# Diagonal state space layer: the kernel matrix last on TensorE, the skip inside the states, block spreading and decay from GpSimd to ScalarE

## The reference, cut to what matters

```
bu_re = jnp.einsum('gpc,bsgc->bsgp', bb_re, uf)
bu_im = jnp.einsum('gpc,bsgc->bsgp', bb_im, uf)
...
_, _, xr, xi = lax.associative_scan(_complex_affine_combine, (a_r, a_i, bu_re, bu_im), axis=1)
y = (jnp.einsum('gcp,bsgp->bsgc', c_re.astype(f32), xr)
     - jnp.einsum('gcp,bsgp->bsgc', c_im.astype(f32), xi)
     + d.astype(f32).reshape(S5_GROUPS, S5_GROUP_CH) * uf)
...
g_a, g_b = jnp.split(jax.nn.gelu(y) @ od_w_glu[o], 2, axis=-1)
x = x + g_a * jax.nn.sigmoid(g_b)
```

## Time and profile before

| | |
|---|---|
| median of 3 runs | 2890.25 us (2887.17 to 2892.11) |
| the profiled execution's own time | 2897.58 us |
| its span, first to last instruction | 2895.8 us |
| busy: PE / DVE / ACT / POOL | 2560.8 / 1790.8 / 922.8 / 1552.7 us |
| the S5 stage, first VectorE product to last state | 2207.08 to 2368.77 us |

### The profile page before, as it was taken

How to read it: one execution, slowest core, us unless ns; L and a number is a source line. 1 busy time by engine, 2 the same in 40 slices (tenths; PEclk the granted TensorE clock), 3 DMA queues, 4 the chain that set the end, 5 groups by cost and what they waited for, 6 DMA issues and landing times.

```text
span 2895.8 us, 36385 instructions
## 1 busy us (share of the span) xinstructions
PE 2560.8 (88%) x12686; PEld 2003.5 (69%) x12686; DVE 1790.8 (62%) x2121; ACT 922.8 (32%) x1317; POOL 1552.7 (54%) x1274
## 2 busy tenths in 40 slices
PE   4978888969999997999588989999995559999998
PEld 3755677747777776778377458888883558888887
DVE  6669855656777675566788556664237763666314
ACT  2023266633444422667312213221022221222102
POOL 4730344535444452445464016766768757767775
PEclk8977899979999997999799689999997889999999
DMA  8846478852233223788431113332240013333222
GB/s 304 271 117 212 160 265 300 303 164 86 82 93 94 94 81 115 275 306 291 138 88 57 62 51 99 90 101 94 95 125 21 22 37 88 102 94 95 95 94 80
DMA packets 319121, 386.72 MB, mean 134 GB/s; under 512 B 51578, under 2 KB 259214, under 8 KB 318902
## 3 DMA queue, kind: packets, MB, share of 16 engines
q1 hardware_dynamic: 261424, 335.84, 35.4%
q10 hardware_dynamic: 34438, 28.08, 3.2%
q0 software_dynamic: 23168, 21.59, 2.3%
HBM read 397.62 MB, written 55.41 MB: 156 GB/s over the span
## 4 chain that ended last, share of the span: by engine, by line
PE 28%; POOL 20%; issue 20%; DVE 15%; DMA 12%; ACT 3%; SPq 1%; ACTq 0%; POOLq 0%; DVEq 0%
POOL WL L829 15%; PE PAIR L527 5%; POOL WH L825 5%; PE PAIR L528 5%; PE PAIR L529 5%; DMA RAW<-in_moe_w 5%; PE PAIR L1830 2%; DMA RAW<-in_ffn_w_up 2%; PE BANK L2260 2%; DVE WL L1932 2%; ACT WH L1750 1%; PE BANK L527 1%; PE BANK L528 1%; PE BANK L529 1%; PE PAIR L1800 1%
## 5 line engine op out<-in xcount | busy, mean ns | idle before, releaser
L829 POOL TENSOR_TENSOR WL<-RAW,WH 128x512 fp32r<-128x512 f32 x584 | 819.2, 1433 | 12.2
L527 PE MATMUL PAIR<-HH,WH 128*128 128x512 f32 x1792 | 714.1, 398 | 51.0 <-POOL HL L1118 30.5
L528 PE MATMUL PAIR<-HL,WH 128*128 128x512 f32 x1792 | 704.8, 393 | 0.0
L529 PE MATMUL PAIR<-HH,WL 128*128 128x512 f32 x1792 | 703.7, 393 | 0.0
L824 POOL TENSOR_TENSOR TURN<-ONES 128x1 f32<-128x1 f32 x146 | 34.6, 237 | 927.3 <-PE PAIR L529 850.4
L527 PEld LDWEIGHTS PAIR<-HH,WH 128*128 128x128 f32 x1792 | 340.3, 190 | 134.9 <-issue 45.0
L529 PEld LDWEIGHTS PAIR<-HH,WL 128*128 128x128 f32 x1792 | 340.5, 190 | 72.0
L528 PEld LDWEIGHTS PAIR<-HL,WH 128*128 128x128 f32 x1792 | 340.6, 190 | 71.3 <-issue 2.4
L825 POOL TENSOR_SCALAR WH<-RAW 128x2048 fp32r<-128x2048 f32 x146 | 281.1, 1925 | 0.0
L1932 DVE TENSOR_TENSOR WL<-RAW,WH 128x2048 fp32r<-128x2048 f32 x78 | 178.7, 2293 | 159.2 <-ACT WH L1750 159.2
L2002 POOL DMA_INDIRECT XG<-htok_scratch,GATHER_I x78 | 142.4, 1825 | 219.1 <-PE PAIR L1800 130.7
(11 more groups left out here) (518 smaller groups left out, 4653.5 us busy)
## 6 DMA issues: line engine op xcount, KB each, us to landing
RAW<-in_moe_w SPq DMA_DIRECT2D x156, 512.0 KB, 4.8
RAW<-in_ffn_w_up SPq DMA_DIRECT2D x88, 512.0 KB, 4.6
W2RAW<-in_moe_w SPq DMA_DIRECT2D x78, 512.0 KB, 6.6
ADA_B<-in_ada_w SPq DMA_DIRECT2D x30, 1024.0 KB, 5.3
RAW<-in_ssm_w_in SPq DMA_DIRECT2D x48, 512.0 KB, 4.9
ADA_A<-in_ada_w SPq DMA_DIRECT2D x18, 1024.0 KB, 7.9
RAW<-in_ffn_w_down SPq DMA_DIRECT2D x32, 512.0 KB, 4.0
RAW<-in_ev_w_in SPq DMA_DIRECT2D x20, 512.0 KB, 4.3
```

Source lines behind the costliest of these rows:

```text
L527: nc.tensor.matmul(o, wh, xh, start=start, stop=False)
L528: nc.tensor.matmul(o, wh, xl, start=False, stop=False)
L529: return nc.tensor.matmul(o, wl, xh, start=False, stop=stop)
L829: ins = pool.tensor_tensor(WL[:, s, c], RAW[:, s, c], WH[:, s, c].bitcast(F32), ALU.subtract)
```

## The change

On TensorE, `pe_s5_prepare` moves the inputs first, then transposes `W1X`, then computes B·u, and puts the kernel matrix last, in the fourth bank. On VectorE, the skip of step k-1 moves from behind the states of step k to a place inside them, between the scans and the last six operations. On GpSimd, sums and differences are taken in place on all 128 partitions (two for `W1_PR`, two for `PRP`), both of which now have two buffers; ScalarE copies them to their blocks (`act_s5_blocks`, eight copies of 64 partitions a step) and also computes `S5_DECAY` (`act_s5_decay`, four activations of 128x128 with a scale per partition). ScalarE's loop is written out. At the start ScalarE does the blocks of steps 0 and 1 before the inputs of step 0.

```
-    PRP = sb("PRP", [P, 4, 4, S5_L + 1, S5_C], F32, r)
-    W1_PR = sb("W1_PR", [P, 4, 4, S5_L, S5_C], F32, r)
+    W1_PR = sb("W1_PR", [P, 2, 4, 4, S5_L, S5_C], F32, r)
...
+    PRP = sb("PRP", [P, 2, 4, 4, S5_L + 1, S5_C], F32, r)
...
 def pool_s5_step(pool, k):
...
+        if k >= 2:
+            pool.e.wait_ge(w["w1x"], k - 1)
+        q = [W1_PR[:, par, i] for i in range(4)]
         for i, (a, b) in enumerate(((br, ar), (bi, ai), (br, ai), (bi, ar))):
-            ins = pool.e.tensor_tensor(W1_PR[:, i], a, b, ALU.mult)
+            ins = pool.e.tensor_tensor(q[i], a, b, ALU.mult)
         pool.link(ins)
-        if k >= 2:
-            pool.e.wait_ge(bank_ready, s5_a(k - 2, 2) + 1)
-        for part, op in ((0, ALU.subtract), (1, ALU.add)):
-            for h in range(2):
-                rows = slice(h * HD, h * HD + HD)
-                ins = pool.e.tensor_tensor(W1X[rows, par, part, :, :, h, :], W1_PR[rows, 2 * part], W1_PR[rows, 2 * part + 1], op)
-        ins.then_inc(w["w1x"], 1)
-        pool.wait(w["w1x"])
+        pool.e.tensor_tensor(q[0], q[0], q[1], ALU.subtract)
+        pool.e.tensor_tensor(q[2], q[2], q[3], ALU.add).then_inc(w["w1_sums"], 1)
+        pool.wait(w["w1_sums"])
...
+        if k >= 2:
+            pool.e.wait_ge(w["ca"], k - 1)
+        q = [PRP[:, par, i] for i in range(4)]
...
+        pool.e.tensor_tensor(q[0], q[0], q[1], ALU.subtract)
+        pool.e.tensor_tensor(q[2], q[2], q[3], ALU.subtract).then_inc(w["ca_sums"], 1)
+        pool.wait(w["ca_sums"])
...
-        pool.e.tensor_tensor(S5_DECAY[:, par], bcast(FIRST[:], 1, 4), bcast(S5K[:, MAG4, tiles], 2, S5_N), ALU.mult)\
-            .then_inc(w["decays"], 1)
...
+    def act_s5_blocks(act, k):
+        w, par = s5_sems, k % 2
+        act.wait(w["w1_sums"])
+        if k >= 2:
+            act.e.wait_ge(bank_ready, s5_a(k - 2, 3) + 1)
+        for part in range(2):
+            for h in range(2):
+                rows = slice(h * HD, h * HD + HD)
+                ins = act.e.activation(W1X[rows, par, part, :, :, h, :], W1_PR[rows, par, 2 * part], ACT.Copy)
+        ins.then_inc(w["w1x"], 1)
+        act.wait(w["ca_sums"])
+        if k >= 2:
+            act.e.wait_ge(bank_ready, s5_y(k - 2) + 1)
+        for part in range(2):
+            for h in range(2):
+                rows = slice(h * HD, h * HD + HD)
+                ins = act.e.activation(CAX[rows, par, part, :, :, h, :], PRP[rows, par, 2 * part], ACT.Copy)
+        ins.then_inc(w["ca"], 1)
+
+    def act_s5_decay(act, k):
+        w, par = s5_sems, k % 2
+        if k >= 2:
+            act.e.wait_ge(w["state"], k - 1)
+        for i in range(4):
+            ins = act.e.activation(S5_DECAY[:, par, i, :], FIRST[:], ACT.Identity, scale=S5K[:, MAG4, 4 * k + i:4 * k + i + 1])
+        ins.then_inc(w["decays"], 1)
...
+        act_s5_decay(act, 0)
+        act_s5_blocks(act, 0)
+        act_s5_blocks(act, 1)
+        act_s5_inputs(act, 0)
+        act_s5_kernel(act, 0)
+        for k in range(KD):
+            if k < KD - 1:
+                act_s5_decay(act, k + 1)
+                act_s5_inputs(act, k + 1)
+            if k:
+                act_s5_gelu(act, None, k - 1)
+            if k < KD - 1:
+                act_s5_kernel(act, k + 1)
+            act_s5_output(act, None, k)
+            if k + 2 < KD:
+                act_s5_blocks(act, k + 2)
+        act_s5_gelu(act, None, KD - 1)
...
 def dve_s5_states(dve, e, k):
...
             ins = dve.e.tensor_tensor_scan(q[i + 1], decay, q[i], 0.0, ALU.mult, ALU.add)
         dve.link(ins)
         if e is not None or k:
+            dve_s5_skip(dve, e, k - 1)
...
             dve_s5_states(dve, e, k)
-            if e is not None or k:
-                dve_s5_skip(dve, e, k - 1)
```

`act_s5_inputs` copies the inputs (bank 0) and the two transposed banks (1 and 2), and `act_s5_kernel` the kernel matrix (bank 3). TensorE's new order, with the waits:

```
+        bank = take_bank(pe, s5_a(k, 0))
...
+        pe.wait(w["w1x"])
         for part in range(2):
+            bank = take_bank(pe, s5_a(k, 1 + part))
...
+        for i in (0, 1, 2):
+            b = s5_a(k, i)
+            pe.e.wait_ge(bank_free[b % 4], b // 4 + 1)
...
+        pe.wait(w["ca"])
+        bank = take_bank(pe, s5_a(k, 3))
```

More of the change, by code:

```diff
@@ L3184, in s5_out @@
         return s5_y(k) + 1
[L3186 to L3194, removed]
     def t2(e, n):
@@ L3285, in pool_s5, with pe_s5_prepare @@
             pool_s5_step(pool, k)
-    def pe_s5_prepare(pe, e, k):
+    def pe_s5_prepare(pe, k):
         w, par = s5_sems, k % 2
+        bank = take_bank(pe, s5_a(k, 0))
+        for i in range(4):
+            for j in range(S5_L):
+                src = HF[:, k:k + 1, :].rearrange("p k (n l) -> p (k n) l", l=S5_L)[:, :, j]
+                ins = nc.tensor.matmul(bank[32 * j:32 * j + 32, i * P:i * P + P], IDENT[:, 32 * i:32 * i + 32], src, start=True, stop=True)
+        ins.then_inc(bank_ready, 1)
         pe.wait(w["w1x"])
         for part in range(2):
-            bank = take_bank(pe, s5_a(k, part), t2(e, 3))
+            bank = take_bank(pe, s5_a(k, 1 + part))
             for i in range(4):
@@ L3296, in pe_s5_prepare @@
             ins.then_inc(bank_ready, 1)
+        pair = take_pair(pe, plan.p["s5"] + k)
+        for i in (0, 1, 2):
+            b = s5_a(k, i)
+            pe.e.wait_ge(bank_free[b % 4], b // 4 + 1)
+        for part in range(2):
+            for i in range(4):
+                ins = nc.tensor.matmul(pair[:, part, i * P:i * P + P], W1_T[:, par, part, i, :], U4[:, par, i, :], start=True, stop=True)
+        ins.then_inc(w["bu"], 1)
         pe.wait(w["ca"])
-        bank = take_bank(pe, s5_a(k, 2), t2(e, 3))
+        bank = take_bank(pe, s5_a(k, 3))
         for i in range(4):
@@ L3303, in pe_s5_prepare @@
         ins.then_inc(bank_ready, 1)
[L3304 to L3317, removed]
     def pe_s5_output(pe, e, k):
@@ L3351, in pe_s5, with act_s5_inputs @@
         pe.wait(h_ready)
[L3353 to L3359, removed]
+        pe_s5_prepare(pe, 0)
         for k in range(KD):
-            step(None, k)
-    def act_s5_prepare(act, e, k):
+            if k < KD - 1:
+                pe_s5_prepare(pe, k + 1)
+            pe_s5_output(pe, None, k)
+    def act_s5_inputs(act, k):
         par = k % 2
         if k >= 2:
-            act.e.wait_ge(bank_ready, t2(e, 12) + (s5_y(k - 2) + 1))
+            act.e.wait_ge(bank_ready, s5_y(k - 2) + 1)
+        b = s5_a(k, 0)
+        act.e.activation(U4[:, par].rearrange("p t n -> p (t n)"), full_bank(act, b)[:], ACT.Copy).then_inc(bank_free[b % 4], 1)
@@ L3369, in act_s5_prepare @@
         for part in range(2):
-            b = s5_a(k, part)
-            bank = full_bank(act, b, t2(e, 3))
+            b = s5_a(k, 1 + part)
+            bank = full_bank(act, b)
             act.e.activation(W1_T[:, par, part].rearrange("p t n -> p (t n)"), bank[:], ACT.Copy).then_inc(bank_free[b % 4], 1)
-        b = s5_a(k, 2)
-        kernel = full_bank(act, b, t2(e, 3))[0:32, :].rearrange("p (t n) -> p t n", n=P)
+    def act_s5_blocks(act, k):
[10 more added lines that the diff above has]
+        if k >= 2:
+            act.e.wait_ge(bank_ready, s5_y(k - 2) + 1)
+        for part in range(2):
+            for h in range(2):
+                rows = slice(h * HD, h * HD + HD)
+                ins = act.e.activation(CAX[rows, par, part, :, :, h, :], PRP[rows, par, 2 * part], ACT.Copy)
+        ins.then_inc(w["ca"], 1)
@@ L3375, in act_s5_prepare, with act_s5_kernel @@
+    def act_s5_decay(act, k):
+        w, par = s5_sems, k % 2
+        if k >= 2:
+            act.e.wait_ge(w["state"], k - 1)
+        for i in range(4):
+            ins = act.e.activation(S5_DECAY[:, par, i, :], FIRST[:], ACT.Identity, scale=S5K[:, MAG4, 4 * k + i:4 * k + i + 1])
+        ins.then_inc(w["decays"], 1)
+    def act_s5_kernel(act, k):
+        par, b = k % 2, s5_a(k, 3)
+        kernel = full_bank(act, b)[0:32, :].rearrange("p (t n) -> p t n", n=P)
         for j in range(S5_L):
@@ L3474, in dve_s5_states @@
         if e is not None or k:
+            dve_s5_skip(dve, e, k - 1)
+        if e is not None or k:
             dve.e.wait_ge(bank_ready, t2(e, 12) + (s5_y(k - 1) + 1))
```

31 lines of the change are left out of this document (7 added, 24 removed).

## The result

The changed kernel takes 2858.09 us (median of 4, 2854.58 to 2863.64) and the kernel before 2890.93 us beside it (median of 4): a ratio of 0.989, 95% interval 0.9872 to 0.9909, 32.8 us less. The forecast was 2855 us, 35.2 us less. In a later set of runs the same pair gave 2857.64 us (6 runs) against 2888.03 us (11 runs), ratio 0.9904 (0.9885 to 0.9922).

A forecast was written before the change was run, and what follows sets the result against it. VectorE, held up by the loop from skip through move and copy to B·u, took 21.9 us a step. Summed steps end the states at 2333.6 instead of 2368.8; 35.2 us off 2890.25 gives 2855 us, range 2846 to 2871.

The forecast's parts named there:

- (a): TensorE order and skip place: the loop skip, move, copy, B·u is cut, so VectorE follows step on step.
- the 0.95 that I gave as a sign: VectorE's busy share between first and last state should exceed 0.95 if the forecast is right.
- My margin for the skip: Output moved back 6.3 us after the previous states; VectorE reaches the skip at 7.0 alone, 9.4 beside busy GpSimd.
- (b): ScalarE's twelve new activations a step take 4.8 us; B·u ends at 12.6 us, hidden behind VectorE's 15.7.
- The lower end of 3.4: Low estimate for ScalarE's twelve new activations, in us, given as eight at 0.28 with their issue overlapping.
- The sum: Adding the stage's steps, last states end at 2333.6 instead of 2368.8: 35.2 us less.
- the 1.04 and 1.25 of my rival: ScalarE's chain sets the pace: at 1.04 us per activation no gain, at 1.25 16 us slower; chance 0.09.
- (c): GpSimd's step falls from 12.9 to 8.4 us alone, so VectorE loses less beside it: steps of 15.7 us.
- GpSimd is not on the chain as a worker: Claim that GpSimd's relief matters only through VectorE, whose steps take 12.29 us beside idle GpSimd, 16.98 beside busy.
- My rival without relief: VectorE loses as much to GpSimd as before: 25.8 us less, 2864 us; chance 0.14.
- (d): GpSimd runs ahead and cuts two weight units beside states 5 and 6, costing VectorE 9 us (8 to 11).
- (e): Stage start: ScalarE does both first block sets before the inputs, so the first product comes 2 us later (0 to 5).

The follow-up runs named there:

- e9: Changed kernel with TensorE's order put back as before, the skip still inside the states: 2863.07 us.
- e10: Changed kernel with the skip put back behind the states, TensorE's new order kept: 2853.08 us.
- e6: Changed kernel, GpSimd cutting after the last states, ScalarE's inputs of step 0 before blocks of step 1, skip three operations later: 2837.73 us.
- e8: Changed kernel without GpSimd's sums of steps 2 to 7, cutting after the last states: 2838.62 us (1 run).
- e3: Changed kernel, with GpSimd waiting for the last states before cutting the gate stage's first two weight units: 2846.75 us.
- e1: Changed kernel with GpSimd's spreading and decay as before and no ScalarE block copies, so the new order alone: 2872.45 us.
- e4: Changed kernel, with ScalarE doing the inputs of step 0 before the blocks of step 1: 2854.67 us.

## Why the prediction was right, step by step

It was right in time, in sign and in the mechanism, a little high in the gain: 35.2 us forecast, 30.9 in the stage. From the end of HF, forecast and measured:

| term | forecast | measured |
|---|---|---|
| first product | 12.3 | 14.8 |
| states of step 0 | 14.8 | 14.4 |
| steps 1 to 4 | 62.8 | 62.0 |
| steps 5 and 6 | 34.6 | 35.1 |
| step 7 | 12.3 | 13.9 |
| last state to gate stage | 7.8 | 8.7 |
| sum | 144.6 | 148.9 |

*(a), the loop.* Right that it is cut and that VectorE then sets the pace in steps 2 to 5; its share of 0.92 over the stage stays under the 0.95 that I gave as a sign. But I took the two edits as one mechanism. e9 and e10 show that either suffices; once TensorE's order is changed, the skip's place leaves the time from T_0 to T_7 as it is. My margin for the skip ("holds, by 0.7 us at the least") failed in steps 1, 6 and 7, where VectorE waited 1.3 to 2.0 us. The 6.3 us to the moved-back output held only at full clock with TensorE free: after idleness the outputs of steps 0 and 5 take 4.6 and 5.5 us for 3.0, and those of step 6 start 2.7 us after T_6, for TensorE still had B·u and the kernel matrix to finish. e6, which asks for the output later, gives step 7 its 1.5 us back.

*(b), ScalarE's twelve.* Forecast 4.8 us, measured 4.9; B·u ends 12.1 us after T_2 and T_3, forecast 12.6; one table load in the stage, as forecast. (The lower end of 3.4 needs all twelve at 0.28 us, not eight.) The estimate from the Trainium skill (ScalarE: Activation LUTs, What ACT_TABLE_LOAD costs) was 3.8; the overlap that it counts between all activations shows in the trace for the decay only, 0.09 us each. The mistake lies in how the chain was thought to act: I compared it with one step of VectorE, B·u against T_(k+1), and left out that it closes on itself over kernel matrix and outputs. That loop, 13.85 us, is the pace of a long run of steps without GpSimd (e8). The sum put steps 6 and 7 of the changed kernel at 12.3. Both wait at the skip for the output: in step 6 because the outputs of step 5 ran at half clock (with them at full clock, e3, it takes 12.8), in step 7 because of the loop. e6 shows that with a later skip neither holds up VectorE. With 6.6 us more in it, 0.96 us per activation on the mean, the kernel is slower than before, sooner than the 1.04 and 1.25 of my rival. It had the right place, and its threshold was too generous because the half clock was not in it.

*(c), GpSimd's relief.* Steps of 15.7 forecast, 15.62 measured: this term was the best. The estimate by the lock between VectorE and GpSimd of the Trainium skill (SBUF — State Buffer, Who interferes with whom) was 15.6; in step 6 of the changed kernel, where GpSimd is all but idle, nearly every operation was back at its time alone, which agrees. But "GpSimd is not on the chain as a worker" was true only of the kernel before. e1 shows that with the loop cut its 17 instructions would have set the pace, so that the relief is worth more than what VectorE loses to contention: 19.3 us from T_0 to T_7 (130.2 - 110.9), of which the later start takes back 7.5 and the end 0.8, so 11.0 of the 30.9 in the stage. My rival without relief had put it at 9.4 (35.2 - 25.8). I had ruled the bound out by looking at the old pace.

*(d), the cutting.* Forecast one step near 20 us, measured 21.3. The change brought the cutting forward by making GpSimd early; before, it lay beside step 6 (27.7 us, with 21.5 for step 5). 10 forecast for steps 5 and 6 together with GpSimd's last step, and 10.0 measured (35.1 us against the 25.1 of e3). No run lets the kernel before wait with the cutting, so how much of that it could have won as well stays open.

*(e), the start.* Two us forecast and 4.5 measured, just inside the range given. Of the 2.5 between them 1.7 are B·u at half clock, 3.75 for 2.04. It is a cost of the order in which ScalarE starts, and e4 takes it off (B·u 2.02 us after a wait of 0.83).

## What to carry to other kernels

When an edit cuts one loop, list every other queue's work per step at the new pace, not at the old: here GpSimd, with 18 us a step beside a busy VectorE (e1), was hidden at 21.9 and would have been the bound at 16. An engine made early does its next job early, and that job may fall beside the bottleneck: one wait put it where VectorE was idle and gave a third as much again as the whole change. And undo the parts of a change one at a time, for of two that do the same only one is needed.

## What the runs showed of the hardware beyond that

In the changed kernel TensorE's half clock cost 1.8 us on B·u of step 0 and 1.6, 2.5 and 2.5 us on the outputs of steps 0, 5 and 7, after waits of 7.8, 3.5, 6.5 and 5.0 us. The length of the last wait alone doesn't tell whether it comes. A kernel matrix in e1_order after a wait of 3.85 us, and the outputs of step 2 in e4_inputs_first after one of 2.27, a row for each:

```profile
2230.19:2232.13 1.94, 1.94 (x17) 1.74 (x17) 1.94 (x4) 0.00 (x0) 1.92 (x2) 1.00 0.77 255
```

```profile
2242.85:2247.10 4.25, 4.25 (x24) 4.02 (x24) 4.06 (x6) 0.00 (x0) 4.17 (x6) 0.65 0.38 123
```

The first ran at full clock; the second, 2.95 us at full clock, fell to half after about a third of its products. No run here isolates what decides it. Small activations issue densely on ScalarE: 64 copies of 64x16 in 7.16 us, 112 ns each, though each is shown as 199 ns long.
